# Two norms behind the feed-forward joined to one root, and the first weight tiles of three stages split a stage earlier

## The chip, the cores and the metric

One core of a Trainium2 chip runs the whole program in one launch. The metric is the device time of one execution in microseconds (us); of several runs the median is given. A time in a row of the trace is counted from the start of the profiled execution's span.

## What is computed

Two transformer blocks of width 1024 over 1024 tokens. The part around the change, cut from the reference:

```python
def rms_norm(x, g):                      # EPS = 1e-6
    y = x * lax.rsqrt(jnp.mean(x * x, axis=-1, keepdims=True) + EPS)
    return y * g

# end of the first block
x = x_mid + gt_f * (jnp.square(jax.nn.relu(modulate(rms_norm(x_mid, g_ffn), sh_f, sc_f) @ w_ff1)) @ w_ff2)
x = rms_norm(x, g_final)

# start of the second block: 16 meta tokens stand ahead of the 1024
h_res = jnp.concatenate([meta, x], axis=1)
for li in range(2):
    h = rms_norm_2(h_res, norm_gain[li])     # same form, same epsilon
    proj = h @ w_in[li]
    ...                                      # Fourier mixer, differential attention, gate
    h_res = h_res + y @ w_out[li]
```

## The kernel before

Activations lie transposed: 128 partitions are 128 features, and the free dimension holds the tokens, so a tensor of 1024 features is eight tile rows of 128 x 1024 (or 128 x 1040 with the 16 meta tokens in front, `L2` = 1040, `META` = 16). `res` (`k.res`) holds the residual. Every matrix product is done in three products of rounded parts: weights and activations are split in a high part (a copy by ScalarE into `..._wh`, `..._hi`) and a low part (a subtraction by VectorE, sometimes GpSimd, into `..._wl`, `..._lo`), and TensorE adds high by high, high by low and low by high in PSUM.

The program is a row of phases. Each phase has one instruction stream per engine (SyncE, ScalarE, TensorE, VectorE, GpSimd), written out by hand in the order in which it runs, with semaphores between them; `phase` ends with a barrier of all engines (L65), so nothing of the next phase starts before the slowest engine of this one has ended. The phases around the change are `wo1` (a call of `mix_out`, which calls `gemm`), `ff` (`feed_forward`), `final_norm`, `pf0` (the first `gemm` of `second_layer`), and, a layer later, `wo20` (again `mix_out`) and `pf1`.

`gemm` makes output tiles in pairs, one per slot s of two. A pair's weights are fetched by SyncE into `raw` (L845), split by ScalarE (`hi`, L887) and VectorE (`lo`, L918), multiplied (L974 and L981, or L960 for the first pair behind a norm), and evacuated. The first pair's raw weights are fetched at the end of the phase ahead by `fetch_first` (L594), which waits until they have landed, and they are split at the start of the phase, ahead of the norm's tiles.

A norm has two halves. The statistics (`square` L637 or `square_at` L654 on ScalarE, `accumulate` L648 or `accumulate_at` L662 on VectorE, `sums` L676 on TensorE with a matrix of ones, `roots` L685 on ScalarE, `reciprocals` L691 on VectorE, `keep` L668, a store of `res` to memory by SyncE) run at the end of the phase that makes the data (`follow`). The tiles (`tiles_dve` L733 and L715, `tiles_act` L707 and L709, `tiles_pool` L715) run at the start of the next, and TensorE takes each tile as it comes.

`feed_forward` runs over 8 groups of hidden features. A group has four units of the first product (kind 1, L2123) and four of the second (kind 2, L2135); a unit of kind 2 gives two tile rows of the output, which VectorE adds to `res` (L2086). The last four units (g = 7, kind 2, u = 0 to 3) stand outside the loop. In unit u the rows 2u and 2u + 1 are made one after the other, in banks of their own.

`final_norm` squares and adds the eight rows of `res` (`n3`), takes the root, scales `res` in place (L789), squares and adds again, now with the meta tokens (`bn0`), takes the second root and its reciprocals, and stores `res` (the second block's output projection reads it back later).

## Time and profile before

| | us |
|---|---|
| median of 3 runs | 2995.29 (2995.28 to 2996.0) |
| the profiled execution | 2999.37 |
| its span | 2997.6 |
| TensorE busy (matmuls) | 2699.0 (90%) |
| VectorE busy | 1256.5 (42%) |
| ScalarE busy | 943.4 (31%) |
| GpSimd busy | 486.9 (16%) |

The page also cuts the span in 40 slices; each digit is the busy share in tenths, and PEclk is the clock that TensorE was granted, in tenths of the full 2.4 GHz:

```profile
PE   4999858899879999999992999989999799998999
DVE  4743552433453333333337422237743522226652
ACT  3412323344242111112203222236731222226640
POOL 0100110342000000000000000018830100007740
PEclk9999978999989999999995999999999899999999
```

In the profile PE is TensorE (PEld its weight loads), DVE VectorE, ACT ScalarE, POOL GpSimd and SP SyncE. A row of a timeline gives the start, the duration, the engine, the line, the operation with output and inputs, how many like it follow one another, and in brackets how long the engine stood idle before it and what released it. The 22nd slice (1574 to 1649 us) holds the end of `ff`, `final_norm` and the start of `pf0`.

### The profile page before, as it was taken

To read this page: it belongs to the slowest core of one execution; us is meant where nothing else is said; L and a number is where in the kernel's file an instruction comes from. 1 tells how busy PE (TensorE), PEld (TensorE's weight loads), DVE (VectorE), ACT (ScalarE), POOL (GpSimd) and SP (SyncE) were. 2 spreads that over 40 slices of the span, in tenths; PEclk is the share of its full clock that TensorE was granted. 3 is DMA by queue.
4 is the path that set the end of the run, shared out by engine and by line. 5 is a ranking of instruction groups with operands and counts; after the bars stand their busy time and mean duration, and the time that the engine had idled before them with its cause. 6 is when DMAs were issued, how large, how long until landed. Compare 5 with 4: busy or idle time off the path is not lost. (4 is left out here: it accounts for less than half of the span.)

```text
span 2997.6 us, 35474 instructions
## 1 busy us (share of the span) xinstructions
PE 2699.0 (90%) x14559; PEld 2306.6 (77%) x14559; DVE 1256.5 (42%) x1592; ACT 943.4 (31%) x1506; POOL 486.9 (16%) x299
## 2 busy tenths in 40 slices
PE   4999858899879999999992999989999799998999
PEld 1777646799758888888882999868888798767887
DVE  4743552433453333333337422237743522226652
ACT  3412323344242111112203222236731222226640
POOL 0100110342000000000000000018830100007740
PEclk9999978999989999999995999999999899999999
DMA  5541001000201111111102114133111213232212
GB/s 218 169 141 41 22 8 50 15 1 1 98 28 57 50 43 49 49 49 49 49 29 86 52 47 100 36 96 72 41 79 71 80 40 85 54 91 61 67 71 85
DMA packets 65518, 189.21 MB, mean 63 GB/s; under 512 B 7776, under 2 KB 26592, under 8 KB 64224
## 3 DMA queue, kind: packets, MB, share of 16 engines
q1 hardware_dynamic: 65376, 187.21, 19.9%
q8 instruction: 101, 1.65, 0.2%
q14 instruction: 41, 0.34, 0.0%
HBM read 146.79 MB, written 16.97 MB: 55 GB/s over the span
## 5 line engine op out<-in xcount | busy, mean ns | idle before, releaser
L1576 DVE TENSOR_REDUCE da_negmax<-ps 128x1 f32<-128x1040 f32 x136 | 167.7, 1235 | 26.1 <-PE ps L1430 19.3
L2086 DVE SCALAR_TENSOR_TENSOR res<-ps,gates,res 128x1024 f32<-128x1024 f32 x64 | 79.2, 1279 | 226.1 <-PE ps L2135 226.1
L1561 POOL TENSOR_TENSOR da_E<-da_E,da_F 128x1040 f32<-128x1040 f32 x68 | 163.8, 2409 | 5.7
L1473 PE MATMUL ps<-da_aT,v 128*128 128x128 f32 (+1 forms) x1224 | 159.1, 276 | 0.7 <-ACT qk L1533 0.7
L2135 PE MATMUL ps<-ff_h_lo,ff_wh 128*128 128x512 f32 x512 | 157.8, 389 | 0.0
L2135 PE MATMUL ps<-ff_h_hi,ff_wh 128*128 128x512 f32 x512 | 157.7, 389 | 0.0
L2135 PE MATMUL ps<-ff_h_hi,ff_wl 128*128 128x512 f32 x512 | 157.7, 389 | 0.0
L2049 ACT ACTIVATE ff_wh<-ff_raw 128x1024 fp32r<-128x1024 f32 x64 | 67.6, 1057 | 284.2 <-PE ps L2135 278.3
L1473 PEld LDWEIGHTS ps<-da_aT,v 128*128 128x128 f32 x1224 | 152.0, 196 | 1.1 <-ACT qk L1533 1.1
L2123 PE MATMUL ps<-ffn_in_hi,ff_wh 128*128 128x512 f32 x480 | 149.4, 393 | 2.2 <-DVE ff_wl L2072 2.2
L2123 PE MATMUL ps<-ffn_in_lo,ff_wh 128*128 128x512 f32 x480 | 149.9, 394 | 0.0
L2123 PE MATMUL ps<-ffn_in_hi,ff_wl 128*128 128x512 f32 x480 | 149.2, 392 | 0.0
L1559 POOL TENSOR_SCALAR da_F<-da_F,da_mixed 128x1040 f32<-128x1040 f32 x68 | 77.3, 1137 | 437.7 <-DVE da_mixed L1587 434.6
L719 POOL MEMSET h_hi<- 128x112 f32 x2 | 0.4, 192 | 863.8 <-POOLq L65 863.8
L2081 DVE TENSOR_TENSOR ff_relu<-ff_relu 128x1024 f32<-128x1024 f32 x32 | 39.2, 1226 | 238.3 <-ACT ff_relu L2060 238.3
L1430 PE MATMUL ps<-st_k,st_q 128*128 128x264 f32 (+3 forms) x408 | 100.6, 356 | 24.3 <-ACT da_E L1528 10.6
L1454 PE MATMUL ps<-ident,da_E 128*128 128x128 f32 x612 | 102.9, 280 | 18.4 <-DVE da_aT L1510 14.6
L2135 PEld LDWEIGHTS ps<-ff_h_hi,ff_wl 128*128 128x128 f32 x512 | 96.1, 188 | 20.1
L2135 PEld LDWEIGHTS ps<-ff_h_lo,ff_wh 128*128 128x128 f32 x512 | 96.1, 188 | 20.1
L2135 PEld LDWEIGHTS ps<-ff_h_hi,ff_wh 128*128 128x128 f32 x512 | 96.1, 188 | 20.0
L2060 ACT ACTIVATE ff_relu<-ps 128x1024 f32<-128x1024 f32 x32 | 32.9, 1027 | 248.2 <-PE ps L2123 241.0
L2123 PEld LDWEIGHTS ps<-ffn_in_hi,ff_wh 128*128 128x128 f32 x480 | 90.7, 189 | 22.1 <-DVE ff_wl L2072 2.7
(462 smaller groups left out, 6243.6 us busy)
## 6 DMA issues: line engine op xcount, KB each, us to landing
ff_raw<-w_ff SPq DMA_DIRECT2D x64, 512.0 KB, 3.2
ada_w<-w_ada SPq DMA_DIRECT2D x16, 1024.0 KB, 7.5
wo_raw<-w_out SPq DMA_DIRECT2D x18, 512.0 KB, 5.1
residual_spill<-res SPq DMA_DIRECT2D x2, 4160.0 KB, 11.2
st_q<-st_q_rounded SPq DMA_DIRECT2D x32, 260.0 KB, 5.1
res<-xT SPq DMA_DIRECT2D x2, 4096.0 KB, 14.1
ada_w<-w_ada SPq DMA_DIRECT2D x4, 2048.0 KB, 26.4
pqk_raw<-w_in SPq DMA_DIRECT2D x16, 512.0 KB, 4.1
```

Of the source, the lines that this page charges most:

```text
L1430: mm = pe.matmul(k.ps[0:rows(g), 3 * (n % 2) + b, a:a + w], q, kk[:, key:key + w], start=(j == 0), stop=(j == 1))
L1454: tr = pe.transpose(k.ps[:, bank(g, b), j * P:(j + 1) * P], E[g % 4][:, t * P:(t + 1) * P], k.ident[:])
L1473: mm = pe.matmul(k.ps[:, pv_bank(g), 0:w], v(g // NQ, t), aT[g % 2][:, t, 0:w], start=(t == 0), stop=(t == NT - 1))
L1559: pool.tensor_scalar(f, f, mixed[:, g % 2:g % 2 + 1], 1.0, ALU.mult, ALU.mult).then_inc(s_F, 1)
L1561: pool.tensor_tensor(e, e, f, ALU.add).then_inc(s_A, 1)
L1576: dve.tensor_reduce(nm[:, n % 4:n % 4 + 1], window(n), AX.X, ALU.max, negate=True).then_inc(s_nm, 1)
L2049: act.activation(wh[:, s, :], raw[:, s, :], ACT.Copy).then_inc(w_hi[s], 1)
L2060: act.activation(rt[:, s, :].rearrange("p (c w) -> p c w", c=2), k.ps[:, 4 * s:4 * s + 2, :], ACT.Relu).then_inc(relu[s], 1)
L2081: dve.tensor_tensor(rt[:, s, :], rt[:, s, :], rt[:, s, :], ALU.mult).then_inc(sqd[s], 1)
L2086: last = dve.scalar_tensor_tensor(out=res[:, m, :], in0=k.ps[:, 4 * s + 2 * t:4 * s + 2 * t + 2, :].rearrange("p c w -> p (c w)"), scalar= ...
L2123: mm = pe.matmul(k.ps[:, 4 * s + c, :], a[:, s, q * P:(q + 1) * P], b(q)[:, o:o + ln], start=(q == 0 and n == 0), stop=(q == KD - 1 and n ...
L2135: mm = pe.matmul(k.ps[:, 4 * s + 2 * t + c, :], a[:, s, e], b[:, par, q, o:o + ln], start=(q == 0 and n == 0), stop=(q == GT - 1 and n == 2))
```

## The change

- `final_norm` and its phase are gone. `JoinedNorm` takes one root for both norms: with x the residual behind the feed-forward, g the final gain and S the mean over features, the product of the two reciprocal roots is 1 / sqrt(S(x² (g² + eps)) + eps²), for the meta tokens 1 / sqrt(S(x²) + eps). Its squares and adds run in the last four units of `ff`, its sums, root and reciprocals at the end of `ff`. The squares and sums of the plain norm (without the gain) run beside them, since the residual itself is still needed.
- The scaling of `res` and its store move into `pf0` (`KeepResidual`): two reciprocals on VectorE ahead of the first `side.dve` unit, eight scalings ahead of the third, and eight stores on SyncE behind the fetch of `pqk0`'s first weights.
- The first weights of `ff`, `pf0` and `pf1` are fetched as before, and split at the end of the phase ahead: high parts on ScalarE ahead of `roots`, low parts on VectorE ahead of `reciprocals` (`split_next` in `gemm`; `split_hi` and `split_lo` in `ff`). TensorE sets the semaphores of those splits itself (`sem_inc`).

The diff, cut to its core:

```diff
+class JoinedNorm(RmsNorm):
+    def join_fetch(self, sp, w_lo, count, raw):
+        for s in (0, 1):
+            sp.wait_ge(w_lo[s], count)
+            sp.dma_start(raw[:, s, :], self.then(s)).then_inc(self.s_w[s], 16)
+    def square_join(self, act, m):
+        act.wait_ge(self.s_x, m + 1)
...
+        act.activation(self.sq_join[m % 2][:, 0:META], self.k.res[:, m, 0:META], ACT.Square)
+        act.activation(self.sq_join[m % 2][:, META:], self.x(m), ACT.Square, scale=self.root[:, m:m + 1]).then_inc(self.s_sqj, 1)
+    def square_x(self, act, m):
...
+        act.activation(self.sq_x[m % 2][:], self.x(m), ACT.Square).then_inc(self.s_sqx, 1)
+    def join_sums(self, pe):
+        pe.wait_ge(self.s_accj, KD)
+        for c, (a, w) in enumerate(self.parts[0]["chunks"]):
+            pe.matmul(ps[:, c, 0:w], self.k.ones[:], self.rstd[0][:, a:a + w], start=True, stop=True).then_inc(self.s_sum, 1)
+        pe.wait_ge(self.s_accx, KD - 1)
+        pe.wait_ge(self.s_sqx, KD)
+        for c, (a, w) in enumerate(self.cx):
+            pe.matmul(ps[:, 4 + c, 0:w], self.k.ones[:], self.rx[:, a:a + w], start=True, stop=False)
+            pe.matmul(ps[:, 4 + c, 0:w], self.k.ones[:], self.sq_x[(KD - 1) % 2][:, a:a + w], start=False, stop=True).then_inc(self.s_sumx, 1)
+    def tiles_dve(self, dve):
...
+                dve.scalar_tensor_tensor(out=z[:, 0:META], in0=self.k.res[:, n, 0:META], scalar=p["gain"](n),
+                                         in1=r[:, 0:META], op0=ALU.mult, op1=ALU.mult)
+                dve.scalar_tensor_tensor(out=z[:, META:L2], in0=self.x(n), scalar=self.both[:, n:n + 1],
+                                         in1=r[:, META:], op0=ALU.mult, op1=ALU.mult).then_inc(self.s_z, 1)
...
+class KeepResidual(Side):
+    def dve(self, dve, m):
+        if m == 0:
+            for a, w in norm.cx:
+                dve.reciprocal(norm.rx[:, a:a + w], norm.rx[:, a:a + w]).then_inc(self.s_r, 1)
+        if m == 2:
+            dve.wait_ge(self.s_r, len(norm.cx))
+            for q in range(KD):
+                dve.scalar_tensor_tensor(out=norm.x(q), in0=norm.x(q), scalar=norm.k.vec[:, V_GFIN + q:V_GFIN + q + 1],
+                                         in1=norm.rx[:], op0=ALU.mult, op1=ALU.mult).then_inc(self.s_scaled, 1)
+    def sp_last(self, sp):
+        for q in range(KD):
+            sp.wait_ge(self.s_scaled, q + 1)
+            sp.dma_start(self.spill[:, q, :], self.norm.k.res[:, q, :]).then_inc(self.s_kept, 16)
+        sp.wait_ge(self.s_kept, 16 * KD)
 def gemm(...):
                 loop(act, body)
+                if split_next:
+                    for s in slots:
+                        act.wait_ge(n_in[s], 16)
+                        act.wait_ge(done[s], NI)
+                        act.activation(wh[:, s, :], n_raw[:, s, :], ACT.Copy).then_inc(n_hi[s], 1)
                 if follow:
                     follow.roots(act, 0)
...
                 loop(dve, body)
+                if split_next:
+                    for s in slots:
+                        dve.wait_ge(n_hi[s], 1)
+                        dve.tensor_tensor(wl[:, s, :], n_raw[:, s, :], wh[:, s, :].bitcast(F32), ALU.subtract).then_inc(n_lo[s], 1)
                 if follow:
                     follow.reciprocals(dve, 0)
 def feed_forward(...):            # ScalarE, last four units (is_end)
+                    if is_end(g, kind) and u == 3:
+                        join.square_join(act, 6)
+                        join.square_x(act, 6)
+                        join.square_join(act, 7)
+                        act.wait_ge(done[s], j + 1)
+                        join.split_hi(act, 1, raw, wh)
+                        join.square_x(act, 7)
+                        join.join_roots(act)
+                        return
                     act.wait_ge(done[s], j + 1)
+                    if is_end(g, kind):
+                        if u == 2:
+                            join.split_hi(act, 0, raw, wh)
+                        else:
+                            hi(s, j + 1)
+                        for m in (2 * u, 2 * u + 1):
+                            join.square_join(act, m)
+                            join.square_x(act, m)
+                        return
...                                # VectorE
-                        dve.wait_ge(done[s], j + 1)
                         for t in range(2):
                             m = 2 * u + t
+                            if is_end(g, kind) and m == 6:
+                                dve.wait_ge(join.s_half, 1)
+                            else:
+                                dve.wait_ge(done[s], j + 1)
                             last = dve.scalar_tensor_tensor(out=res[:, m, :], ...)
+                            if is_end(g, kind) and m == 6:
+                                join.add_join(dve, 6)
+                                join.add_x(dve, 6)
...
                     if not is_last(g, kind, u):
                         lo(s, j + 1)
+                    if is_end(g, kind):
+                        for m in ((2 * u, 2 * u + 1) if u < 3 else (7,)):
+                            join.add_join(dve, m)
+                            if m < KD - 1:
+                                join.add_x(dve, m)
+                        if u >= 2:
+                            join.split_lo(dve, u - 2, raw, wh, wl)
+                        if u == 3:
+                            join.join_reciprocals(dve)
-    final_norm(nc, k, n3, follow, (k.res[:, :, 0:META], d["metaT"]), ("pf0", rows(d["w_in2"]), KD * P, 2))
```

## Rows read from the trace of the kernel before

**Rows 1.** Windows view, the hole behind the feed-forward; columns as named in the fence.
```profile
core 0: us, PE busy (x) PEld busy (x) DVE busy (x) ACT busy (x) POOL busy (x), PEclk, DMA share, GB/s
1578.50:1639.40 60.90, 7.62 (x10) 3.03 (x10) 49.52 (x37) 23.99 (x25) 0.32 (x2) 0.53 0.28 105
```
**Rows 2.** Timeline, all engines, from the last feed-forward update to `pf0`.
```profile
1578.54 2.48 DVE L2086 SCALAR_TENSOR_TENSOR res<-ps,gates,res 128x1024 f32<-128x1024 f32 x2 [8.40 <-PE ps L2135]
...
1595.50 0.69 ACT L685 ACTIVATE n_rstd<-ps,vec 128x512 f32<-128x512 f32 x1 [3.74 <-PE ps L676]
...
1597.21 0.69 ACT L685 ACTIVATE n_rstd<-ps,vec 128x512 f32<-128x512 f32 x1 [1.02 <-PE ps L676]
...
1621.50 3.84 PE L676 MATMUL ps<-bn_acc,ones 128*128 128x348 f32 x6 [24.33 <-DVE bn_acc L648]
...
1623.65 6.68 DVE L691 RECIPROCAL bn_rstd<-bn_rstd 128x348 f32<-128x348 f32 x3 [2.20 <-ACT bn_rstd L685]
...
1632.29 2.00 ACT L887 ACTIVATE pf_wh<-pf_raw 128x1024 fp32r<-128x1024 f32 x2 [6.37 <-PEq L65]
...
1635.66 2.51 DVE L733 SCALAR_TENSOR_TENSOR bn_z<-res,vec,bn_rstd 128x1040 f32<-128x1040 f32 x2
...
1639.48 1.21 PE L960 MATMUL ps<-h_hi,pf_wh 128*128 128x348 f32 x3 [14.15 <-DVE h_lo L715]
```
**Rows 3.** Timeline, the end of `wo1` and the start of `ff`.
```profile
852.84 1.28 ACT L685 ACT_TABLE_LOAD   x1
...
855.29 0.69 ACT L685 ACTIVATE n_rstd<-ps,vec 128x512 f32<-128x512 f32 x1 [1.17 <-PE ps L676]
856.01 6.57 DVE L691 RECIPROCAL n_rstd<-n_rstd 128x512 f32<-128x512 f32 x2 [1.94 <-ACT n_rstd L685]
...
863.42 2.00 ACT L2049 ACTIVATE ff_wh<-ff_raw 128x1024 fp32r<-128x1024 f32 x2 [5.89 <-PEq L65]
...
866.79 2.48 DVE L733 SCALAR_TENSOR_TENSOR n_z<-res,a,n_rstd 128x1024 f32<-128x1024 f32 x2
```
**Rows 4.** Waits of SyncE and timeline, the end of `wo20` and `pf1`.
```profile
SPq L824 <- DMA residual_spill<-res: 10.9, 1, 10.9
...
2320.04 6.68 DVE L691 RECIPROCAL bn_rstd<-bn_rstd 128x348 f32<-128x348 f32 x3 [2.20 <-ACT bn_rstd L685]
...
2328.92 2.00 ACT L887 ACTIVATE pf_wh<-pf_raw 128x1024 fp32r<-128x1024 f32 x2 [6.61 <-PEq L65]
...
2332.29 2.51 DVE L733 SCALAR_TENSOR_TENSOR bn_z<-res,vec,bn_rstd 128x1040 f32<-128x1040 f32 x2
```
**Rows 5.** Timeline, VectorE behind unit 2 of the last feed-forward group.
```profile
1567.66 2.48 DVE L2086 SCALAR_TENSOR_TENSOR res<-ps,gates,res 128x1024 f32<-128x1024 f32 x2 [7.27 <-PE ps L2135]
```
**Rows 6.** Windows view, for the granted clock (PEclk, third number from the end).
```profile
1578.50:1593.30 14.80, 0.00 (x0) 0.00 (x0) 11.71 (x10) 8.24 (x8) 0.00 (x0) 0.63 0.25 76
1639.40:1643.00 3.60, 3.52 (x12) 3.55 (x13) 3.60 (x4) 1.12 (x2) 1.27 (x1) 0.50 0.02 9
1643.00:1648.00 5.00, 5.00 (x32) 5.00 (x31) 5.00 (x3) 2.11 (x2) 2.20 (x1) 0.92 0.00 0
...
2100.00:2200.00 100.00, 95.99 (x763) 88.88 (x762) 73.18 (x102) 68.66 (x140) 81.52 (x48) 1.00 0.13 31
```
**Rows 7.** Timeline, ScalarE, a table load elsewhere and the operation behind it.
```profile
281.99 1.28 ACT L491 ACT_TABLE_LOAD   x1
283.29 0.21 ACT L491 ACTIVATE ret_tmp<-ret_tmp 128x12 f32<-128x12 f32 x1
```
**Rows 8.** Timeline, VectorE and ScalarE in `pf0`.
```profile
1665.22 1.23 DVE L918 TENSOR_TENSOR pf_wl<-pf_raw,pf_wh 128x1024 fp32r<-128x1024 f32 x1 [8.40 <-ACT pf_wh L887]
1667.21 1.23 DVE L918 TENSOR_TENSOR pf_wl<-pf_raw,pf_wh 128x1024 fp32r<-128x1024 f32 x1 [0.77 <-ACT pf_wh L887]
...
1688.36 1.16 ACT L1004 ACTIVATE ya<-ps 128x348 f32<-128x348 f32 x3 [10.25 <-PE ps L981]
```
**Rows 9.** Waits of SyncE from 1560 to 1720: total, times, longest.
```profile
SPq L824 <- DMA pqk_raw<-w_in: 5.1, 1, 5.1
```
**Rows 10.** DMA issues: times, size of one, median us to landing.
```profile
out_T<-res SPq DMA_DIRECT2D x8, 512.0 KB, 2.8
```

More of the change, by code:

```diff
@@ L744, in wait_tile @@
             pe.wait_ge(self.s_plo, pool)
-def final_norm(nc, k, norm, follow, load, then):
-    src, gain = norm.parts[0]["src"], norm.parts[0]["gain"]
-    with phase(nc):
-        norm.open_stats()
-        follow.open_stats()
-        s_in, s_x = k.sem("meta_in"), k.sem("final_x")
-        with nc.Block() as block:
-            @block.sync
-            def _(sp):
-                sp.dma_start(*load).then_inc(s_in, 16)
-                sp.wait_ge(s_in, 16)
-                fetch_first(sp, k, then)
-                follow.keep(sp)
-            @block.scalar
-            def _(act):
-                for q in range(KD):
-                    norm.square(act, q)
-                norm.roots(act, 0)
-                act.wait_ge(s_in, 16)
-                for q in range(KD):
-                    act.wait_ge(s_x, q + 1)
-                    follow.square(act, q)
-                follow.roots(act, 0)
-            @block.tensor
-            def _(pe):
-                norm.sums(pe, 0)
-                follow.sums(pe, 0)
-            @block.vector
-            def _(dve):
-                for q in range(KD):
-                    norm.accumulate(dve, q)
-                norm.reciprocals(dve, 0)
-                dve.wait_ge(norm.s_rstd, norm.chunks_before(1))
-                for q in range(KD + 1):
-                    if q < KD:
-                        dve.scalar_tensor_tensor(out=src(q), in0=src(q), scalar=gain(q), in1=norm.rstd[0][:],
-                                                 op0=ALU.mult, op1=ALU.mult).then_inc(s_x, 1)
-                    if q:
-                        follow.accumulate(dve, q - 1)
-                follow.reciprocals(dve, 0)
@@ L2949, in second_layer @@
     gemm(nc, k, f"pf{li}", rows(d["w_in2"], R0), 4, KD, XH, XL, cx, evac_act=copy_out(tile(ya), cx), preloaded=True,
-         norm=norm, then=(f"pqk{li}", rows(d["w_in2"], R0 + 4 * P), KD * P, 2))
+         norm=norm, split_first=k.split[f"pf{li}"], side=KeepResidual(norm, spill) if li == 0 else None,
+         then=(f"pqk{li}", rows(d["w_in2"], R0 + 4 * P), KD * P, 2))
     gemm(nc, k, f"pqk{li}", rows(d["w_in2"], R0 + 4 * P), 8, KD, XH, XL, cx, evac_act=copy_out(tile(qk), cx),
@@ L2984, in second_layer @@
         follow = layer_norm(k, 1, spill)
-        more = dict(follow=follow, then=("pf1", rows(d["w_in2"], 20 * P), KD * P, 2))
+        more = dict(follow=follow, then=("pf1", rows(d["w_in2"], 20 * P), KD * P, 2), split_next=True)
     else:
```

151 lines of the change are left out of this document (129 added, 22 removed).

## The prediction

> **What bounds the kernel now.** The page's forty slices come first: TensorE is at its full rate almost everywhere, so time can only be won where it stands still. The windows and the timeline around each norm show where. The longest hole lies between the last feed-forward matmul and the first matmul of `pf0`: 60.9 us in which TensorE works 7.62 [rows 1]. The reader follows that hole from one row to the next in [rows 2]: the last two updates of `res` start at 1578.54, the first norm's roots at 1595.50 and 1597.21, the second norm's sums start at 1621.50, its three reciprocals run from 1623.65 for 6.68, the next phase begins at 1632.29, the first `bn_z` at 1635.66, TensorE at 1639.48. All of it is one serial chain through VectorE, ScalarE and TensorE. The holes ahead of `ff` and `pf1` have the same last part: after the phase begins, ScalarE and VectorE split two weight tiles before VectorE reaches its first tile of the norm (863.42 to 866.79 in [rows 3], 2328.92 to 2332.29 in [rows 4]).
>
> **The joined norm.** It removes the whole `final_norm` phase: eight squares and adds, a root, eight scalings, eight more squares and adds, a second root. What stays is a tail behind the last unit of `feed_forward`. I work it out on the clock of the trace before. A last-group unit takes 10.88 us on TensorE (1567.66 to 1578.54 [rows 2, 5]); units 0 and 1 of the group get their squares and adds under the next unit: VectorE has two updates (2.48), a weight split and four adds (five two-input operations at 1.23 [rows 8]), 8.6 us, and ScalarE a split, four squares and two 16-wide squares, 5.6 us. Both fit, and the PSUM release and the weight splits that TensorE waits for stand ahead of the adds. Cost on the path: nothing; without that cover it would be a square and an add, about 2.2 us, for each row of `res`.
> Unit 2 ends at 1567.66. VectorE updates rows 4 and 5 until 1570.1. ScalarE splits the first weights (2.00 for two [rows 3], so about 1.0) and squares row 4 by 1570.3. Four adds and one low part, five times about 1.18 as they overlap a little, end at 1576.2; the update of row 6 ends at 1577.4. Its half of the matmuls was done at 1573.1, so VectorE is the later one. Then the chain alternates: the 16-wide square (0.21 is what a 12-wide operation takes [rows 7]) and the square of row 6 to 1578.8, two adds to 1581.2, update of row 7 to 1582.4 (TensorE was done at 1578.5), its square to 1583.8, its add to 1585.1. The second weight split fits between that and the first reciprocal.
> From there the old second norm repeats: the first reciprocal starts 2.15 after the first sum, and the three take 6.68 [rows 2]: VectorE ends at 1593.9. The next phase began 0.84 after the last reciprocal (862.58 to 863.42 [rows 3]): 1594.8. With the weights split already, VectorE starts its tiles there; from the first `bn_z` to TensorE it was 3.82 [rows 2]. Each tile now has a 16-wide part of its own, at most 0.21 and at least nothing; two of them precede the first low part, I take 0.16 in all. TensorE starts at 1598.8 instead of 1639.48: 40.7 us saved.
> The sums for the plain norm are new on TensorE and ScalarE: four matmuls behind the three joined ones, so from 1588.9. In the old hole a 512-wide chunk took 1.71 (1595.50 to 1597.21) at a granted 0.50, the 1.2 GHz level; at the 2.4 GHz level half of that, 0.86. Four take 3.4 to 6.8 and end at 1592.3 to 1595.7, and the last root about 1.1 later, at 1593.4 to 1596.8. VectorE ends at 1593.9, so the price is 0 to 2.9. TensorE will have stood still since 1578.5 and start at the lower level, as [rows 6] shows for that stretch (0.63 on average, so it falls within it). When `pf0` started after a long pause it was granted 0.50 up to 1643.0 and 0.92 on average over the next 5 us, in unbroken work from 1639.48 [rows 2, 6]. The joined sums are 3.84 of such work, so I take one cold chunk and three fast ones: 1594.3 at the end, 0.4 later than VectorE. I take 0.3 off: 40.4 saved.
>
> **The residual moves into `pf0`.** Two reciprocals on VectorE (about 6.6, as the three took 6.68) stand between the last tile and the low part of the third weight tile. VectorE stood idle for 8.40 between the last tile and that low part at 1665.22 [rows 8]; it is what is queued behind the reciprocals, and TensorE wants it only at the end of its unit, behind all products with the high weights. Cost nothing. Then eight scalings (1.24 each, 2.48 for two) run from 1668.4 (1667.21 plus 1.23 [rows 8]) to 1678.3 beside matmuls; nothing is queued behind them, as `pf0` is evacuated by ScalarE. On SyncE the eight stores stand behind the fetch for `pqk0`, whose landing it waited for 5.1 [rows 9], after two issues behind 1668.4: from 1674.4. The one large store took 10.9 of waiting [rows 4]: 1685.3. The phase ends with the evacuation at 1688.36 plus 1.16 [rows 8], 1689.5, so 4.2 us of cover is left. The other bound is eight stores end to end at the 2.8 of a 512 KB store [rows 10]: 22.4, ending 1696.8, 7.3 late. I take the first, because nothing waits between the stores. The range of this part is 0 to 7.3. The fetch itself is not moved behind them. The early load of the 16 meta columns is one issue on SyncE ahead of weight fetches that are not due for 30 us: nothing.
> A rule of the Trainium skill speaks against this part: DMA: Bandwidth & Descriptors, Rules for kernel authors, wants at least 1 MiB per transfer for full bandwidth and small ones joined. The store of 4160 KB becomes eight of 520 KB. By the rule they run below the large one's rate; no row shows how far, and the sum would not change until they were a third slower.
>
> **The splits ahead.** Ahead of `pf1`: ScalarE makes two high parts after the last square, VectorE two low parts before the reciprocals. No table load stands there, and the roots keep their place within 0.2 us. The old phase did not begin with the reciprocals (2320.04 plus 6.68 is 2326.72) but at 2328.92, after SyncE had waited 10.9 for the store [rows 4]. So the delay costs nothing and the store is still late there. VectorE's first tile moves from 2332.29 to 2328.92: 3.4 saved. Without the wait for the store it would be 0.8 to 2 more or less; the store is not touched, so I take none.
> Ahead of `ff` the store does not exist and the delay counts. The table load for the root ran from 852.84 right behind the last square, the root waited for TensorE until 855.29 [rows 3]. Now two high parts (2.00) come first: load 854.84 to 856.12, root at 856.13, 0.84 late; the reciprocals end at 863.4, the phase begins at 864.26 and the first tile starts there instead of at 866.79: 2.5 saved. The two low parts end at 856.4, before the reciprocals can start, so they add nothing. `pf0`'s own split is in the 40.4.
> The rule that bears on this: in the trace the operation behind another load starts 1.30 after the load does (281.99 to 283.29 [rows 7]), so the load costs its own 1.28. The Trainium skill, ScalarE: Activation LUTs, What ACT_TABLE_LOAD costs, gives 1283 ns and a drain of some 1380 ns more. By it the root of `ff` would come at 857.5, this part would save 1.1, not 2.5, and the result would be 2950.4.
> In both cases the tiles behind the start keep their spacing, since TensorE ran without a gap on them before; in `pf0` the 16-wide parts use at most 1.7 us of a lead that is over 2 us at the third tile.
>
> **Sum.** 40.4 + 3.4 + 2.5 = 46.3. The profiled execution took 2999.37 (span 2997.6 and 1.8 around it) and becomes 2953.1. The median of the runs is 4.1 below the profiled one: 2995.29 less 46.3 is 2949.0.
>
> **The rivals.**
> The plain norm's sums and roots end the feed-forward phase. For it: TensorE is certainly slow when it starts, and the joined sums of before never saw the faster level. Against it: work goes on unbroken. Price 2.9 instead of the 0.3: 2951.6. Chance 0.18.
> The stores end `pf0`. For it: the transfers are eight and small. Against it: 4.2 us of cover, no wait between them. Price up to 7.3, a middle of 3.5: 2952.5. Chance 0.08.
> The table load has a drain: 2950.4, chance 0.06.
> The splits ahead do not do what they say: something else than the weights holds VectorE's first tile, so 5.9 us are not won: 2954.9. Against it: in both phases VectorE's first tile follows directly on the second low part. Chance 0.03.
> Slower than before: ScalarE, VectorE and the matmuls now work together in the last feed-forward group and in `pf0`, and the granted clock falls there to the 1.2 GHz level. Four units of 10.88 would take 43.5 us more and the 45 us of `pf0` at the faster level as much again, 42 us slower in all: 3037. It decides from the point where over 46 us of matmul work lose the faster level. Against it: between 2100 and 2200, VectorE, ScalarE and GpSimd work 73, 69 and 82 us of 100 beside the matmuls, and the granted clock is 1.00 [rows 6]. Chance 0.02. A part of it that only cancels the gain: 0.01, 2995.
>
> **How the numbers follow.** The likeliest, 2949.0, has 0.62. The range: down by 3, if the tail's semaphore steps are quicker, the clock rises earlier and TensorE has not yet cooled at 1585 (half of the 1.15 of a chunk); up to 2955.0, which takes in the cold sums, the drain, the missing splits and the lower half of the stores. Less than 2 in 10 is outside 2946.0 to 2955.0. A measurement of this kernel can tell about 0.2%, 6 us, from no change. Faster has all cases but the last two: 0.97; same 0.01, slower 0.02.
>
> **What would show it.** Right: no phase between `feed_forward` and `pf0`; the joined sum starts some 6.6 us after the last feed-forward matmul; TensorE's pause there is about 20 us between the last matmul and `pf0` (sums included) instead of 61; the first operation of VectorE in `ff`, `pf0` and `pf1` is a tile of the norm; the phase ahead of `pf1` still begins with the store. Wrong: a root of the plain norm behind the last reciprocal; SyncE waiting for `residual_spill` when `pf0`'s last evacuation is over; a gap on TensorE inside `ff`'s last group, or a granted clock under 1.0 there.

## The result

| | us |
|---|---|
| kernel before, same chip (4 runs) | 2995.28 (2994.91 to 2996.0) |
| changed kernel (4 runs) | 2947.18 (2946.21 to 2948.08) |
| ratio | 0.9834, 95% interval 0.9822 to 0.9845 (the two medians alone give 0.9839) |
| its profiled execution, and its span | 2946.21, 2944.4 |

The change saves 48.1 us by these medians; the forecast's sum was 46.3. The forecast was right on where the time lies. It was 1.8 us short on the size by the medians. By the ratio, 0.9834, the changed kernel takes 2945.6 against the base of 2995.29, which is 0.4 below the forecast's lower edge of 2946.0; by its own median it is 1.2 above that edge. The profile after, its slices first (the kernel before has the same rows in the table ahead of the change):

```profile
PE   4999867899879999999998999989998899998899
DVE  4743553433453333333338512337743522226752
ACT  3412323344333112221114222147731222226640
POOL 0100110332100000000001000028820100007740
PEclk9999988999989999999999999999999999999999
```

The slice with a granted clock of 0.5 is gone. The timeline of the same stretch as [rows 2], from the third unit of the last feed-forward group to `pf0` (L2241 is the update of `res`, L2308 the feed-forward's matmuls, L1093 `pf0`'s first ones):

```profile
1563.42 2.48 DVE L2241 SCALAR_TENSOR_TENSOR res<-ps,gates,res 128x1024 f32<-128x1024 f32 x2 [2.69 <-PE ps L2308]
...
1573.65 0.61 PE L2308 MATMUL ps<-ff_h_hi,wo_wl 128*128 128x512 f32 x2
...
1576.65 1.28 DVE L2241 SCALAR_TENSOR_TENSOR res<-ps,gates,res 128x1024 f32<-128x1024 f32 x1
...
1578.09 1.13 ACT L798 ACTIVATE join_sq<-res,join_root 128x1024 f32<-128x1024 f32 x1
...
1579.25 1.24 DVE L814 TENSOR_TENSOR join_rstd<-join_rstd,join_sq 128x1040 f32<-128x1040 f32 x1 [1.32 <-ACT join_sq L798]
...
1580.55 3.83 PE L837 MATMUL ps<-join_rstd,ones 128*128 128x348 f32 x6 [6.29 <-DVE join_rstd L814]
...
1582.69 6.68 DVE L858 RECIPROCAL join_rstd<-join_rstd 128x348 f32<-128x348 f32 x3 [1.07 <-ACT join_rstd L848]
...
1584.17 1.36 PE L841 MATMUL ps<-join_rstd_x,ones 128*128 128x512 f32 x2
...
1588.14 0.69 ACT L852 ACTIVATE join_rstd_x<-ps,vec 128x512 f32<-128x512 f32 x1 [1.03 <-PE ps L842]
...
1590.36 0.23 DVE L870 SCALAR_TENSOR_TENSOR bn_z<-res,vec,join_rstd 128x16 f32<-128x16 f32 x1 [0.99 <-PEq L65]
...
1594.43 1.20 PE L1093 MATMUL ps<-h_hi,wo_wh 128*128 128x348 f32 x3 [6.33 <-DVE h_lo L715]
```

The reader follows the chain as in [rows 2]: TensorE ends the feed-forward at 1574.26, the joined sums start at 1580.55, the reciprocals end at 1589.37, VectorE's first operation in `pf0` is a tile of the norm, and TensorE starts at 1594.43. The hole is 20.1 us long instead of 60.9. The last root of the plain norm ends at 1588.83, ahead of the last reciprocal. The windows of the changed kernel over this hole and its parts show the clock:

```profile
1574.30:1594.40 20.10, 7.56 (x14) 3.66 (x15) 16.67 (x15) 9.28 (x13) 0.33 (x2) 0.76 0.14 48
1580.50:1584.00 3.50, 3.45 (x6) 2.18 (x7) 2.43 (x2) 1.71 (x3) 0.00 (x0) 0.50 0.00 0
1584.00:1588.00 4.00, 4.00 (x9) 1.48 (x7) 4.00 (x3) 1.24 (x2) 0.00 (x0) 0.90 0.00 0
```

The joined sums run at 0.50, the 1.2 GHz level, and the plain ones behind them mostly at the 2.4 GHz level (0.90 on average), as forecast. The start of `ff` and that of `pf1`, against [rows 3] and [rows 4]:

```profile
851.80 1.99 ACT L1039 ACTIVATE wo_wh<-ff_raw 128x1024 fp32r<-128x1024 f32 x2
...
853.80 1.28 ACT L685 ACT_TABLE_LOAD   x1
855.10 1.48 ACT L685 ACTIVATE n_rstd<-ps,vec 128x512 f32<-128x512 f32 x2
855.82 6.57 DVE L691 RECIPROCAL n_rstd<-n_rstd 128x512 f32<-128x512 f32 x2 [0.40 <-ACT n_rstd L685]
...
863.28 2.48 DVE L733 SCALAR_TENSOR_TENSOR n_z<-res,a,n_rstd 128x1024 f32<-128x1024 f32 x2 [0.90 <-PEq L65]
```
```profile
2283.77 2.52 DVE L733 SCALAR_TENSOR_TENSOR bn_z<-res,vec,bn_rstd 128x1040 f32<-128x1040 f32 x2 [2.34 <-PEq L65]
```

Both phases begin with a tile. Ahead of `pf1`, VectorE has been idle for 2.34 us: there SyncE still waits 10.9 us for the store, as in [rows 4]. Ahead of `ff` it is 0.90.

A table of stages says more than one pair of profiles, because the same code doesn't take the same time twice. Its marks are VectorE's first tile of `ff`, of `pf0` and of `pf1`, VectorE's first weight split in the phase behind `pf0`, the first maximum of the next attention, and the start of the last two additions to `res`. The last column runs from there to the end of the execution.

| profile | to `ff` | to `pf0` | `pf0` | to `pf1` | to attention | to last add | to end |
|---|---|---|---|---|---|---|---|
| before | 866.79 | 768.87 | 55.76 | 640.87 | 365.37 | 294.04 | 7.67 |
| before, e8 | 864.54 | 766.93 | 55.12 | 644.18 | 364.76 | 294.21 | 7.64 |
| before, e16 | 864.70 | 766.93 | 55.09 | 640.18 | 365.24 | 294.47 | 7.64 |
| before, e17 | 864.84 | 766.94 | 55.09 | 640.05 | 365.35 | 294.07 | 7.65 |
| before, e18 | 862.45 | 766.89 | 55.11 | 643.25 | 365.52 | 294.71 | 7.67 |
| changed | 863.28 | 727.08 | 55.94 | 637.47 | 365.22 | 290.54 | 6.68 |
| changed, e9 | 864.77 | 728.32 | 55.37 | 640.94 | 364.61 | 293.87 | 6.68 |
| changed, e13 | 861.76 | 727.42 | 55.78 | 637.29 | 365.22 | 293.83 | 6.67 |
| join alone, e4 | 864.50 | 728.07 | 55.85 | 640.54 | 365.41 | 293.91 | 6.68 |
| join alone, e14 | 863.79 | 728.12 | 55.85 | 640.53 | 365.39 | 290.60 | 6.68 |
| store in `pf1`, e11 | 862.32 | 727.07 | 55.93 | 636.28 | 363.70 | 293.74 | 6.69 |

### The profile page after: what moved, and what is told of

It reads as the page before. It is cut to its first block and busy times, and to the rows that moved or that the text cites. A ratio compares the mean times of both kernels' runs of the same rounds, so it can differ in the third digit from the quotient of the medians.

```text
span 2944.4 us, 35494 instructions
## 1 busy us (share of the span) xinstructions
PE 2695.1 (92%) x14563; PEld 2303.3 (78%) x14563; DVE 1255.9 (43%) x1601; ACT 943.6 (32%) x1516; POOL 486.9 (17%) x299
## 5 line engine op out<-in xcount | busy, mean ns | idle before, releaser
L2241 DVE SCALAR_TENSOR_TENSOR res<-ps,gates,res 128x1024 f32<-128x1024 f32 x64 | 79.3, 1279 | 209.6 <-PE ps L2308 209.6
L2308 PE MATMUL ps<-ff_h_lo,wo_wh 128*128 128x512 f32 x512 | 157.8, 389 | 0.0
L2308 PE MATMUL ps<-ff_h_hi,wo_wh 128*128 128x512 f32 x512 | 157.7, 389 | 0.0
L2308 PE MATMUL ps<-ff_h_hi,wo_wl 128*128 128x512 f32 x512 | 157.7, 389 | 0.0
L2296 PE MATMUL ps<-ffn_in_hi,wo_wh 128*128 128x512 f32 x480 | 149.4, 392 | 2.2 <-DVE wo_wl L2225 2.2
L2296 PE MATMUL ps<-ffn_in_lo,wo_wh 128*128 128x512 f32 x480 | 149.8, 394 | 0.0
L2296 PE MATMUL ps<-ffn_in_hi,wo_wl 128*128 128x512 f32 x480 | 149.3, 392 | 0.0
L2308 PEld LDWEIGHTS ps<-ff_h_hi,wo_wl 128*128 128x128 f32 x512 | 96.1, 188 | 20.2
L2308 PEld LDWEIGHTS ps<-ff_h_lo,wo_wh 128*128 128x128 f32 x512 | 96.1, 188 | 20.0
L2308 PEld LDWEIGHTS ps<-ff_h_hi,wo_wh 128*128 128x128 f32 x512 | 96.1, 188 | 20.0
L2296 PEld LDWEIGHTS ps<-ffn_in_hi,wo_wh 128*128 128x128 f32 x480 | 90.6, 189 | 22.1 <-DVE wo_wl L2225 2.7
```

The source lines that it names most:

```text
L2241: last = dve.scalar_tensor_tensor(out=res[:, m, :], in0=k.ps[:, 4 * s + 2 * t:4 * s + 2 * t + 2, :].rearrange("p c w -> p (c w)"), scalar= ...
L2296: mm = pe.matmul(k.ps[:, 4 * s + c, :], a[:, s, q * P:(q + 1) * P], b(q)[:, o:o + ln], start=(q == 0 and n == 0), stop=(q == KD - 1 and n ...
L2308: mm = pe.matmul(k.ps[:, 4 * s + 2 * t + c, :], a[:, s, e], b[:, par, q, o:o + ln], start=(q == 0 and n == 0), stop=(q == GT - 1 and n == 2))
```

## The experiments

### Each split undone, and all three

e1 takes back the split of `ff`'s first weights, e2 that of `pf1`'s, e3 that of `pf0`'s, e4 all three. The edits, cut to their core:

```diff
# e1: mix_out of layer 1 (the call's end), and the splits back at the start of ff
-    ... then=("ff", rows(d["w_ff"]), KD * P, 2), split_next=True)
+    ... then=("ff", rows(d["w_ff"]), KD * P, 2))
...
+                hi(0, 0)      # ScalarE, ahead of norm.tiles_act; VectorE likewise with lo
+                hi(1, 0)
# e2: wo20
-        more = dict(follow=follow, then=("pf1", rows(d["w_in2"], 20 * P), KD * P, 2), split_next=True)
+        more = dict(follow=follow, then=("pf1", rows(d["w_in2"], 20 * P), KD * P, 2))
# e3: the last units of feed_forward
-                        join.split_hi(act, 1, raw, wh)
...
-                            join.split_hi(act, 0, raw, wh)
...
-                        if u >= 2:
-                            join.split_lo(dve, u - 2, raw, wh, wl)
```

> The changed kernel, but the first weights of ff are split at the start of ff again. My theory (the two low parts stood ahead of VectorE's first tile, and the table load costs no more than its 1.28): 2.5 us slower than the changed kernel, about 2949.7, and the first tile of ff 3.4 after the phase begins. Rival (a drain behind the load, by the Trainium skill, ScalarE: Activation LUTs, What ACT_TABLE_LOAD costs): only 1.1 slower, 2948.3. Rival (something else held the first tile): within 0.5.

> The changed kernel, but the first weights of pf1 are split at the start of pf1 again. My theory: the store of the residual still sets where pf1 begins, so all 3.4 us of the split come back, 2950.6. Rival (the split ahead delayed the reciprocals and cost part of its gain): 2.5 or less, 2949.7.

> The changed kernel, but the first weights of pf0 are split at the start of pf0 again, and no longer in the tail of ff. My theory: 3.4 come back at the start of pf0; in the tail VectorE loses one low part between the updates of rows 5 and 6 (1.14), which takes that much off: 2.3 slower, 2949.5. Rival (the split in the tail is free because row 6 is not ready earlier): 3.4 slower, 2950.6.

> The changed kernel with all three pairs of first weights split at the start of their phases again: the joined norm and the moved residual alone. My theory (the parts add up): 2.5 + 3.4 + 2.3 = 8.2 slower than the changed kernel, 2955.4, and so 39.9 faster than before. Rival (the parts interact through the granted clock: a pause of TensorE shorter by a few us leaves it at the 2.4 GHz level): a sum that differs from the three single ones by over 1.5 us.

| | median (us) | ratio to before |
|---|---|---|
| e1, `ff` | 2952.42 | 0.9854 (0.9839 to 0.9869) |
| e2, `pf1` | 2951.24 | 0.9844 (0.9831 to 0.9858) |
| e3, `pf0` | 2952.53 | 0.9852 (0.9838 to 0.9865) |
| e4, all three | 2954.89 | 0.9859 (0.9844 to 0.9874) |

The medians lie 4.1 to 5.4 us above the changed kernel's 2947.18 for each part and 7.7 for all three: they don't add up. They also come from another chip, on which the kernel before took 2996.45, 1.2 us more than beside the changed kernel. The traces add up. Each is measured from the end of the last matmul ahead of the stage to VectorE's first tile in it. The changed kernel needs 13.98 us there ahead of `ff`, 16.09 ahead of `pf0` and 15.05 ahead of `pf1`. e1 needs 16.56, so it has lost 2.6; e2 18.27, which is 3.2 more; e3 18.34, which is 2.25 more. e3's tail is 1.1 shorter, as VectorE has one low part less there, and its start 3.3 longer. Its rows, in which the two low parts stand ahead of the first tile again (the last matmul ends at 1574.02):

```profile
1581.36 6.68 DVE L858 RECIPROCAL join_rstd<-join_rstd 128x348 f32<-128x348 f32 x3 [2.20 <-ACT join_rstd L848]
1590.09 2.36 DVE L1047 TENSOR_TENSOR pf_wl<-ff_raw,pf_wh 128x1024 fp32r<-128x1024 f32 x2 [2.05 <-ACT pf_wh L1010]
1592.37 0.23 DVE L870 SCALAR_TENSOR_TENSOR bn_z<-res,vec,join_rstd 128x16 f32<-128x16 f32 x1
```

That is 8.1 together, and e4 loses the same 2.6, 2.3 and 3.2 at the same three places. So e1 to e3 bear out the theory of each at its own place, and their rivals fall there. What is left of the differences lies in stages that the edits don't touch. e1 loses nothing more in `ff` and even gets 1.3 back there, which is the next point. In the last stage all three take 2.9 to 3.3 us more than the first profile of the changed kernel. But the changed kernel takes as much itself when it is run again (293.8 in e9 and e13 against 290.5). One window of that stage, the first profile of the changed kernel and then e13, shows that the granted clock differs there with the same code:

```profile
2728.00:2748.00 20.00, 17.22 (x134) 16.09 (x135) 12.90 (x19) 13.87 (x29) 14.04 (x9) 1.00 0.19 42
```
```profile
2728.00:2748.00 20.00, 17.36 (x125) 16.23 (x123) 11.82 (x18) 12.24 (x25) 12.34 (x8) 0.91 0.19 41
```

What e1 gets back. TensorE stops for 2.25 us behind the first unit of `ff`. The timeline of TensorE there, e1 first, then the changed kernel; two matmuls of 512 columns are one row:

```profile
895.99 0.72 PE L2300 MATMUL ps<-ffn_in_hi,ff_wh 128*128 128x512 f32 x2 [2.25 <-DVE ff_wl L2228]
...
897.02 0.62 PE L2300 MATMUL ps<-ffn_in_hi,ff_wl 128*128 128x512 f32 x2
897.47 0.62 PE L2300 MATMUL ps<-ffn_in_hi,ff_wh 128*128 128x512 f32 x2
```
```profile
894.22 0.73 PE L2296 MATMUL ps<-ffn_in_hi,wo_wh 128*128 128x512 f32 x2 [2.24 <-DVE wo_wl L2225]
...
896.01 1.05 PE L2296 MATMUL ps<-ffn_in_hi,wo_wh 128*128 128x512 f32 x2
896.86 1.05 PE L2296 MATMUL ps<-ffn_in_lo,wo_wh 128*128 128x512 f32 x2
897.72 1.05 PE L2296 MATMUL ps<-ffn_in_hi,wo_wl 128*128 128x512 f32 x2
```

The pause is the same, but in the changed kernel the pairs soon behind it take 1.05 us for some 3.4 us, and in e1 0.62. This is no draw of luck alone. In all twelve profiles in which `ff`'s weights are split early (three of them with the unread matmuls of e7, e10 and e12), the granted clock of the 20 us around that place is 0.91 to 0.92. Of the eight in which they aren't (five of the kernel before, e1, e4, e14) only the first profile of before shows it, the others 1.00. What of the earlier start brings it about, no run shows. From `ff`'s first tile to its last matmul it costs 1.2 us (709.8 in e1 and e8, 711.0 in the changed kernel). So of the 2.6 us that the split brings at the first tile, about half is given back 30 us later.

### The plain norm left out, the stores one by one

```diff
# e5: join_sums and join_roots without the plain norm
-        for c, (a, w) in enumerate(self.cx):
-            pe.matmul(ps[:, 4 + c, 0:w], self.k.ones[:], self.rx[:, a:a + w], start=True, stop=False)
# e6: KeepResidual.sp_last
             sp.dma_start(self.spill[:, q, :], self.norm.k.res[:, q, :]).then_inc(self.s_kept, 16)
+            sp.wait_ge(self.s_kept, 16 * (q + 1))
```

> The changed kernel without the plain norm's four sums and two roots in the tail of ff (left out, so the stored residual is scaled wrongly). My theory (the three joined reciprocals end the phase): from the last feed-forward update to the first tile of pf0 nothing changes, 0.0 to 0.2 us. Rival (the plain sums and roots end the phase): that stretch gets 0.5 to 2.9 us shorter.

e5 took 2946.85 (ratio 0.9834, 0.982 to 0.9848), the same as the changed kernel. From the feed-forward to `pf0` it took 727.14 us against 727.08. The plain norm's sums cost nothing, and the rival that gave them 2.9 us falls.

> The changed kernel, but each of the eight stores in pf0 is issued only when the one before has landed. My theory (a 520 KB store alone takes about 2.8 and the eight end 3.5 ahead of the end of pf0 when they overlap): they end 8 x 3.1 = 25 after the first issue, the next phase begins some 9 later, 2956. Rival (the stores hardly overlap now, their issues being 1.2 apart): within 2 of the changed kernel.

e6 took 2956.86 (0.9865, 0.9851 to 0.988). `pf0` took 62.09 us instead of 55.94, so waiting for each store costs 6.15 us. SyncE's waits from 1560 to 1720, the changed kernel first, then e6 (total, times, longest), and its issues in e6:

```profile
SPq L940 <- DMA residual_spill<-res: 4.2, 1, 4.2
SPq L903 <- DMA pqk_raw<-w_in: 3.5, 1, 3.5
SPq L940 <- PEq L940: 3.5, 1, 3.5
```
```profile
SPq L903 <- DMA residual_spill<-res: 15.7, 7, 2.2
...
SPq L940 <- DMA residual_spill<-res: 2.3, 1, 2.3
```
```profile
1629.76 18.84 SPq L903 DMA_DIRECT2D residual_spill<-res  x8
```

In the changed kernel the wait for the stores is over 3.5 us before the other engines are done (the third row). One by one they need 6.15 + 3.5 = 9.7 us more. The median came out where it was expected (2956), but in part by luck: the expectation had the next phase 9 us later, and it is 6.15, as the stores end 21 us after the first issue and not 25. The rest of the median lies in other stages. So the stores were hidden by 3.5 us, and this is how near the part is to a loss: 6 of the 7.3 us that the forecast gave to stores end to end came about as soon as a wait stood between them.

### TensorE kept busy in its pauses

```diff
+def keep_busy(pe, k, bank, n):      # unread matmuls with the ones
+    for _ in range(n):
+        pe.matmul(k.ps[:, bank, :].rearrange("p (a b) -> p a b", b=P), k.ones[:], ...)
# e7: n = 3 to 7 around the sums and at the start of ff, pf0 and pf1
# e10: n = 1 to 6, and each group behind a step of the norm, as
+                    pe.wait_ge(follow.s_rstd, len(follow.parts[0]["chunks"]) - 1)
+                    keep_busy(pe, k, 7, 3 if len(follow.parts[0]["chunks"]) == 2 else 2)
```

> The changed kernel with matmuls whose result nobody reads in TensorE's pauses around ff, pf0 and pf1 (4 to 7 at a time, on a free PSUM bank), so that the granted clock stays at the 2.4 GHz level. My theory (a start from a pause costs half of the 3.5 us that it runs at the 1.2 GHz level, and the first joined sum comes 0.6 earlier): 3 x 1.7 + 0.6 = 5.7 faster than the changed kernel, 2941.5. Rival (the tiles of the norm, not TensorE, set the pace of the first product): under 2 us. Rival (the extra matmuls hold up the ones that count): slower.

> As the earlier run with unread matmuls in TensorE's pauses, but now each group of them is tied to a step of VectorE's chain (the norm's root, the joined root, the split's high half), and there are few of them, so that none can hold up a real matmul: at the ends of layer 1's and layer 2's output projection, ahead of and behind the joined sums, and at the start of the feed-forward and of the two projections behind norms. Their results are read by nothing. Theory (the cold start behind each pause costs 0.5 to 1.7 us, and the earlier run lost it again by dummies that ran late): 3 to 5 us faster than the changed kernel on this chip, some 2942 to 2944. Rival A (the records show a clock gained at those places and lost again at others, so that the sum is nothing): within 1 us of the changed kernel. Rival B (the dummies themselves cost): slower by 2 to 4 us as in the earlier run.

e7 took 2951.34 (0.985, 0.9837 to 0.9862), 4 us more than the changed kernel; e10 2948.73 (0.9841, 0.9826 to 0.9856), no difference. In e7 the hole is shorter, 19.5 us at full clock, but at the start of `ff` the unread matmuls themselves ran cold and held up the real one, which starts 6.3 us behind the first tile of the norm instead of 5.0:

```profile
864.96 6.23 PE L749 MATMUL ps<-ones 128*128 128x512 f32 x10 [2.72 <-PEq L65]
870.62 1.03 PE L2298 MATMUL ps<-ffn_in_hi,wo_wh 128*128 128x512 f32 x2
```

Tied to the norm's steps (e10), they hold up no real matmul. Against the changed kernel `pf0` gets 1.4 us shorter (54.58) and the stretch from `pf1` to attention 3.3 (361.90), but the feed-forward takes 2.2 more (729.29) and the stretch from `pf0` to `pf1` 3.1 more (640.55). The expected 3 to 5 us didn't come. In this kernel unread matmuls didn't buy off the start at the lower clock: what they gain at the start of a stage isn't seen in the whole.

### The same kernels again

> The kernel before, unchanged, as an experiment. My theory (single executions differ by several us, because TensorE starts from some ten pauses and the moment at which its granted clock rises is not fixed by the program): ratio 1.000, an interval of 0.001 or more, runs between 2994 and 3002, and a profile whose pauses in the second attention have another granted clock than in the first one. Rival (the 1.8 us by which my forecast missed are a property of the change): runs within 1 us of 2995.3.

> The changed kernel unaltered, once more, beside the kernel before on the same chip. It measures how far the result itself moves between executions. Theory (the 1.8 us by which the result lies under the forecast's sum is within the spread of TensorE's granted clock from one execution to the next): median 2945 to 2951, single executions differing by several us, and a saving against the runs of the kernel before on this chip of 46 to 50 us. Rival (the sum missed a real gain of about 2 us): the saving stays at 48 us or more in nearly all executions.

The kernel before against itself gave 0.9996 (0.9987 to 1.0005). Its runs lay between 2992.63 and 3000.2 us, those of the changed kernel in e9 between 2947.21 and 2954.56, median 2948.67 (0.9837). So one execution can be 7 us off another of the same program, more than any single term but the join. On its chip e9 saves 49.2 us (2997.91 to 2948.67), within the 46 to 50 that its theory expected; that doesn't rule out the rival of a real gain of about 2 us that the sum missed.

> The changed kernel unaltered, the reference for the two below on one chip. Theory A (the size of a term was missed: the whole saves 48 us or more on every chip): saving 48 to 50 us against the runs of the kernel before on this chip. Theory B (chance of the granted clock): 45 to 48 us here.

> The join alone, with the three early splits undone, beside the whole and the kernel before on one chip. The forecast's terms: 40.4 us faster than before, 5.9 us slower than the whole; the traces of the single parts added up to 8.2 us for the three splits (2.6, 3.4 and 2.2) and 40.8 less 2.2 for the join with its first splits undone, 38.6. If the excess of the result over the sum sits in the splits, this kernel is 8 us slower than the whole and 40 us faster than before; if it sits in the join, 6 us slower than the whole and 42 us faster than before.

e13 took 2947.96 (0.9841), e14 2953.67 (0.986), the kernel before on that chip 2996.18. The whole saves 48.2, the join alone 42.5, the three splits 5.7. The expectation put 6 us for the splits beside an excess in the join, and 8 beside an excess in the splits. The 5.7 are nearer to the first, but drawing the five and four runs again gives -0.5 to 9.6, so these runs don't decide it. By the traces the splits bring 8.1, of which `ff` gives 1.2 back. The join without its first splits shortens the feed-forward's stage by 38.8 us (766.93 to 728.1) and lengthens `pf0` by 0.7. That is 38.1 of the 42.5, and 1.0 more is the end of the run, described below. The rest isn't located, and it needn't be a gain, as the 42.5 have an interval of 38.7 to 45.5.

> The kernel before, unaltered, for its profile. The code from pqk0 to pf1's first tile is the same in both kernels up to the two splits; it took 640.87 and 644.18 us in the two profiles of the kernel before, and 637.3 to 640.9 in those of the changed kernel. Theory (the join leaves TensorE with a better granted clock further on): 643 to 644 here in most profiles, and a start of ff as in the others. Rival (each execution draws its own dips): 640.9 in most.

> The same kernel, a second profile: 643 to 644 us in that stretch by the theory, 640.9 by the rival. For the stretch of ff up to its last matmul: 709.8 or 711.7 us, the former where the pause behind the second unit doesn't cost TensorE its clock.

> The same kernel, a third profile, with the same two numbers to read. From da1 to the end it took 294.0 and 294.2 us in the two profiles so far, while the changed kernels took 290.6 in some and 293.8 in others: 290.6 in one of the three would show that this step too is drawn by chance.

One execution each: 2994.25, 2993.99 and 2995.6 us. The shared stretch from `pf0` to `pf1` took 640.2, 640.1 and 643.3: two levels, drawn anew from one execution to the next, as the rival said. The stretch of the feed-forward took 766.9 in all three; the first profile, from which the forecast was made, is the odd one with 768.87. From attention to the last addition none of the five profiles of before shows the 290.6 that two of the six joined ones in the table do. Of all fifteen joined profiles it is three (e7 has 290.9), too few to call that systematic.

One term is systematic, and it stands in the last column of the table: from the last additions to the end of the execution it is 7.64 to 7.67 us in all five profiles of before and 6.67 to 6.69 in all fifteen with the join. SyncE's last wait shows it, before first, then the changed kernel:

```profile
SPq L824 <- DMA out_T<-res: 3.2, 1, 3.2
```
```profile
SPq L940 <- DMA out_T<-res: 2.3, 1, 2.3
```

The last store of the output, 512 KB as before, lands 0.9 us sooner. Nothing in the change touches it, and no run here tells why.

### A store moved into `pf1`

```diff
-side=KeepResidual(norm, spill) if li == 0 else None,
+side=KeepResidual(norm, spill) if li == 0 else StoreHere(k, (spill, k.res[:])),
# StoreHere issues the 4160 KB store first in the phase and waits for it last
```

> The store of layer 1's residual (4160 KB) is issued at the start of the second layer's output projection's successor, the projection pf1, and waited for at its end, instead of being issued behind the output projection and holding SyncE ahead of pf1. Theory (the 10.9 us wait for that store set when pf1 began, by 1.0 to 1.3 us): pf1 begins 1.0 to 1.3 us earlier than in the changed kernel, and the run is faster by that. Rival (VectorE's norm and TensorE's last matmuls set the beginning, the store was covered): within 0.3 us at pf1's first matmul.

> The changed kernel with the store of layer 1's residual inside pf1, once more beside the changed kernel itself. Theory (the store set pf1's beginning by 1.2 us, as the last run's trace shows at VectorE's first tile there): 1 to 1.5 us faster than the changed kernel on this chip. Rival (the 2.9 us between the medians of the last call was mostly chance and the gain at pf1's beginning is given back): equal within 0.5 us.

e11 took 2945.73 (0.9827, 0.9813 to 0.984) and e15 2945.32 (0.9828, 0.9814 to 0.9841). The ten runs together have a median of 2945.4, the fourteen of the changed kernel 2948.0, and the difference of 2.5 has a 95% interval of 1.7 to 3.3 by drawing the runs again. VectorE's first tile in `pf1`, in e11:

```profile
2281.60 2.51 DVE L733 SCALAR_TENSOR_TENSOR bn_z<-res,vec,bn_rstd 128x1040 f32<-128x1040 f32 x2 [1.10 <-PEq L65]
```

It stands idle 1.10 us ahead of that tile instead of 2.34: the 1.24 us that the store held it. A further 1.5 us came between `pf1` and attention in both runs (363.7 against 365.2), where the granted clock of one pause, between 2580 and 2600, is 0.91 instead of 0.83. So this version beats both kernels, by 1.2 us through its mechanism and by 1.5 through the granted clock in TensorE's pauses. That the second follows from the earlier start is argued, not shown.

> The two before it together: unread matmuls in TensorE's pauses, tied to steps of the norm's chain, and the store of layer 1's residual inside pf1. If both theories hold, 4 to 6 us faster than the changed kernel on this chip (about 2941 to 2943); if only the store sets something, 1 us faster; if neither, no difference.

e12, e10 and e11 together, had a median of 2944.51, but runs from 2943.78 to 2959.42 (0.9841, 0.9821 to 0.9861). It was expected 4 to 6 us below the changed kernel if both theories held; its median is 4.2 below that of e9 on the same chip. With such a spread it isn't told apart from e11, and e10 gives no reason to expect more.

## Why the prediction was right or wrong

**The step that failed** is the range, and with it a term of the sum. The forecast let the time fall only by 3 us, and all its reasons for that lie in the hole behind the feed-forward. It put the end of the run and the stages behind `pf0` at nothing, and took its base from one median. The hole came out as forecast. What the runs show in place of the nothing is 0.97 us gained at the last store in every profile with the join, 3 us and more by which single stages with the same code differ from one execution to the next, and a base 0.9 us higher than the one it used. In the sum the mis-sized term is the split ahead of `ff`: 2.5 forecast, 2.6 less 1.2 measured. The parts follow.

**The hole: right.** Forecast 40.7 less 0.3 for the plain roots, measured 40.8. The steps agree one by one: the first joined sum starts 6.3 us behind the last feed-forward matmul (6.6), reciprocals 6.68 (6.68), the phase 0.99 behind them (0.84), TensorE 4.07 behind the first tile (3.98). The last units of the group showed no gap on TensorE (27.20 us busy of the 27.20 up to 1574.2). Of the 0.3 for cold sums nothing was needed: the last plain root ended 0.54 us ahead of the last reciprocal, not 0.4 behind. e5 confirms it.

**The residual in `pf0`: right.** Hidden, with 3.5 us of cover instead of 4.2. SyncE needed 7.88 us to issue the eight stores, the last at 1635.4. The rule from the Trainium skill (DMA: Bandwidth & Descriptors, Rules for kernel authors) shows little here: from the first store's issue at 1628.80 to the end of the wait at about 1640.9 the eight of 520 KB took 12.1 us, where the one of 4160 KB took 11.2 from issue to landing in the kernel before. So they were 0.9 us slower together, not the third that would have mattered.

**The split ahead of `pf1`: right.** 3.4 forecast; 3.2 from the last matmul ahead of it to VectorE's first tile (18.29 to 15.05), and 3.2 in e2. The stage behind `pf0` gives 2.9 to 3.4, according to the pair of profiles (640.87 to 637.47, 640.18 to 637.29). That the store was still late there is shown by e11.

**The split ahead of `ff`: right at its place, wrong in its sum.** 2.5 forecast, 2.6 measured at the first tile. The step that failed is the sentence that the tiles behind the start keep their spacing because TensorE ran without a gap: it looked at the first unit alone. 30 us later there is a pause of 2.25 us, and with the earlier start TensorE's clock falls behind it. That gives back about 1.2. The pause stands in the kernel before too (2.23 to 2.25 us in its five profiles); there the clock fell behind it only in the profile from which the forecast was made. The drain of the table load that the Trainium skill states (ScalarE: Activation LUTs, What ACT_TABLE_LOAD costs) didn't show: the root starts 1.30 us after the load does (853.80 to 855.10), as in [rows 7], and that rival falls.

**The end: missed.** The 0.97 us of the last store stood in no term. Why it lands sooner stays open.

**The base and the range: too narrow.** The sum was taken off one median of three runs that happened to lie within 0.8 us of one another, and the range got no term for how far executions of one program differ. The 63 runs of the kernel before, the first profiled one aside, have a median of 2996.2 and reach from 2992.25 to 3004.38; the fourteen of the changed kernel 2948.0 and 2946.21 to 2954.56. Their difference is 48.2 us, with a 95% interval of 47.2 to 49.7 by drawing the runs again. The means differ by 47.6, with an interval of 46.1 to 49.0.

The terms as they were measured are 2.6 - 1.2 for `ff`, 41.1 for the hole up to VectorE's first tile (40.8 up to TensorE's start), 3.2 for `pf1`, 0.97 for the end, and -0.6 for `pf0`. Of these 0.6 a quarter of a microsecond is the two parts of 16 elements ahead of TensorE's start; for the rest, the kernel before usually regains its clock sooner (0.71 over the first 5 us in e8, 0.59 in the changed kernel). They come to 46.1. So the forecast's 46.3 was near the sum of what can be located, partly by luck, because a missed gain and a missed loss cancel. Some 2 us of the measured gain stay open by the medians; by the means it is 1.5, and their interval reaches down to the 46.1. No profile places these 2 us at the change. The profiles differ by as much, and more, in stages that both kernels share, with one of two times from run to run (640 or 643 to 644 us, 290.6 or 293.8). Whether the change moves the odds of those levels isn't settled.

**The rivals.** Cold sums: no (e5). Stores that end `pf0`: no, but e6 shows that they would by 6 us. A drain: no. The splits that don't do what they say: no (e1 to e4). The clock falling to the lower level in the last group or in `pf0`: no, it is 1.00 from 1563.4 to 1574.3 and from 1599.4 to 1619.4, where `pf0` has left its start at the lower level.

## What to carry to other kernels

Where one serial chain of small steps stands between two stages of matmuls, its length can be forecast within 1 us from the chain's own rows; what can't is the rest of the run. Before a term of 2 or 3 us is trusted, look for the pauses of TensorE behind it, since its clock behind the same pause can change with the start of the stage (twelve of twelve against one of eight here), and take several profiles of the kernel before: one of five was odd by 2 us in the very stage that was changed. A wait for a store at the end of a phase is worth moving into the next phase where it holds VectorE's first tile back, as it did by 1.2 us here.

## What was not expected of the hardware

- The same pause of 2.24 us behind `ff`'s first unit cost TensorE its clock in twelve of twelve profiles where the weights were split early, and in one of eight where they weren't.
- The fifth and the eighth tile's part of 16 elements (L870), each issued while GpSimd worked on a low part, took 2.41 and 2.42 us instead of 0.23. The forecast had put each at 0.21 at most. Each ended with GpSimd's operation, some 0.03 us behind it (1600.44 and 1600.40 in the rows below). The fifth did so in all fifteen profiles with the join, the eighth in three. VectorE's lead over TensorE covered both. The rows of the changed kernel:

```profile
1596.81 3.59 POOL L715 TENSOR_TENSOR h_lo<-bn_z,h_hi 128x1040 fp32r<-128x1040 f32 x1 [6.17 <-ACT h_hi L709]
...
1598.03 2.41 DVE L870 SCALAR_TENSOR_TENSOR bn_z<-res,vec,join_rstd 128x16 f32<-128x16 f32 x1
```

- The output's last store landed 0.9 us sooner in every profile with the join, with nothing changed at it.
